# Attention of five tiles set 1 to 8 slots earlier in a hand-written schedule, with the resident routing weights

## What is computed

```
x += W_out[ diffattn(4 heads) | multi-scale pool ](rmsnorm(x) @ W_in)
x += PEER(rmsnorm(x))     # 8 heads, each: top 16 of 128*128 experts per token
x += sigmoid(rmsnorm(x) @ W_gate) * (p @ W_ple);  y = rmsnorm(x)
# PEER, for the indices idx that the routing scores choose:
h = gelu(einsum('td,thkd->thk', xb, u_tab[idx]))
out = einsum('thk,thkd->td', gate * h, v_tab[idx])
```

## Time and profile before

| | |
|---|---|
| Median of the three runs | 3161.15 us |
| Profiled execution, its own time | 3163.01 us |
| Its span, first to last instruction | 3160.7 us |
| PE / DVE / ACT / POOL busy | 74 / 71 / 30 / 42 % |
| DMA moved | 1260.27 MB, mean 399 GB/s |
| of it by the gather queue | 1133.76 MB, 87.2 % of 16 engines' time |
| of it by SyncE's queue | 122.82 MB |
| TensorE clock granted, mean | 0.870 |

### The profile page before, as it was taken

How to read it: one execution, slowest core, us unless ns; L and a number is a source line. 1 busy time by engine, 2 the same in 40 slices (tenths; PEclk the granted TensorE clock), 3 DMA queues, 4 the chain that set the end, 5 groups by cost and what they waited for, 6 DMA issues and landing times.

```text
span 3160.7 us, 53314 instructions
## 1 busy us (share of the span) xinstructions
PE 2345.9 (74%) x20876; PEld 935.8 (30%) x20876; DVE 2237.4 (71%) x5470; ACT 943.7 (30%) x2421; POOL 1319.9 (42%) x1143
## 2 busy tenths in 40 slices
PE   8789999577876877757876767576777676667656
PEld 4633333233333333213432222122222222222112
DVE  1466777668778789656667667587777777777775
ACT  1312333234435345222322212122332322222222
POOL 1024344334444334335555544344444444544442
PEclk9999999788898889878888888788898887889878
DMA  7679999999999999999999999999999999999996
GB/s 273 217 318 420 421 410 421 416 414 383 406 403 418 409 409 403 414 408 417 417 417 411 416 417 400 418 406 418 413 419 408 419 418 421 404 420 417 420 417 270
DMA packets 202034, 1260.27 MB, mean 399 GB/s; under 512 B 24048, under 2 KB 27400, under 8 KB 60848
## 3 DMA queue, kind: packets, MB, share of 16 engines
q0 software_dynamic: 159808, 1133.76, 87.2%
q1 hardware_dynamic: 40540, 122.82, 10.0%
q10 hardware_dynamic: 1436, 0.29, 0.0%
HBM read 1228.31 MB, written 28.65 MB: 398 GB/s over the span
## 4 chain that ended last, share of the span: by engine, by line
DMA 29%; PE 14%; DVE 8%; issue 3%; POOL 3%; DVEq 2%; ACT 2%; another core or an unknown queue 0%; POOLq 0%; ACTq 0%
DMA ring<-in_uv,idx 29%; PE sc L1007 7%; DVE ring L1887 4%; PE sc L1040 3%; POOL ring L2104 2%; PE route L982 1%; PE sc L1009 1%; DVEq L1897 1%; ACT diag L1402 1%; POOL front L2120 0%; ACT hgelu L1397 0%; PE sc L906 0%; DVE x L1936 0%; PE sc L1000 0%; PE sc L876 0%
## 5 line engine op out<-in xcount | busy, mean ns | idle before, releaser
L2104 POOL DMA_INDIRECT ring<-in_uv,idx x1056 | 1241.0, 1175 | 1647.6 <-PE sc L1009 1426.8
L1007 PE MATMUL sc<-ring,diag 32*32 32x512 f32 x8192 | 1232.3, 721 | 680.7 <-ACT diag L1402 617.6
L1887 DVE CUSTOM_DVE_ANT_0 ring<-ring,xn_cur 128x1024 f32<-128x1024 f32 x1056 | 1280.4, 1222 | 639.6 <-DMA ring<-in_uv,idx 604.1
L1009 PE MATMUL sc<-ring,diag 32*32 32x512 f32 x8192 | 1237.2, 721 | 0.0
L1007 PEld LDWEIGHTS sc<-ring,diag 32*32 32x32 f32 x8192 | 272.9, 117 | 1452.4 <-ACT diag L1402 1018.3
L1397 ACT ACTIVATE hgelu<-hdot 128x2 f32<-128x2 f32 x528 | 107.5, 204 | 1820.6 <-DVE hdot L1887 1740.3
L1402 ACT ACTIVATE diag<-gate_d,hgelu 128x32 f32<-128x32 f32 x1056 | 281.8, 314 | 21.2
L1009 PEld LDWEIGHTS sc<-ring,diag 32*32 32x32 f32 x8192 | 273.6, 117 | 5.8 <-issue 4.8
L564 PE MATMUL sc<-big,front 128*128 128x512 f32 x384 | 176.9, 604 | 3.3 <-DVE front L1515 2.9
L1397 ACT ACT_TABLE_LOAD x128 | 164.2, 1283 | 2.2
L982 PE MATMUL route<-big,xnT 128*128 128x256 f32 x560 | 134.4, 395 | 0.0
(11 more groups left out here) (310 smaller groups left out, 2362.9 us busy)
## 6 DMA issues: line engine op xcount, KB each, us to landing
front<-wqk_scratch SPq DMA_DIRECT2D x21, 1024.0 KB
ring<-in_uv,idx POOLq DMA_INDIRECT x1056
big<-in_w_in SPq DMA_DIRECT2D x8, 1024.0 KB, 13.7
wqk_scratch<-front SPq DMA_DIRECT2D x8, 1024.0 KB, 4.9
big<-wqk_scratch SPq DMA_DIRECT2D x8, 1024.0 KB
x<-x_scratch SPq DMA_DIRECT2D x12, 512.0 KB
ring<-in_wq_t POOLq DMA_DIRECT2D x10, 512.0 KB, 13.8
front<-in_x SPq DMA_DIRECT2D x8, 512.0 KB
```

What stands on the lines that cost most here:

```text
L1007: pe.matmul(sc[own, 0, :], diag[own, r, :], uv_rows[own, r, D:D + W4], start=opens_sum, stop=closes).then_inc(row_added[r], 1)
L1009: pe.matmul(sc[other, 1, :], diag[own, r, :], uv_rows[own, r, D + W4:2 * D], start=opens_sum, stop=closes).then_inc(row_added[r], 1)
L1887: dve.tensor_tensor_reduce(uv_rows[:, k % RING, 0:D], uv_rows[:, k % RING, 0:D], xn_cur[:, :], 1.0, 0.0, ALU.mult, ALU.add, hdot[:, n % 2, ...
L2104: pool.indirect_dma_start(uv_rows[:, k % RING, :], None, uv, bass.IndirectOffsetOnAxis(ap=idx[:, n % PH, j:j + 1], axis=0)).then_inc(row_i ...
```

## The change

The bases of tiles 3 to 7 go from 84, 101, 123, 145, 167 to 83, 99, 119, 139, 159: tile 3 follows tile 2 by 16 slots instead of 17, tile 4 follows tile 3 by 16 instead of 17, and tiles 5, 6 and 7 follow by 20 instead of 22. With tile 7, `BACK_FREE` goes from slot 190 to 182, and `C0` and all slots of the samples' attention by 8. `STREAMED` goes from 29 to 28, so head 28 is read from the resident weights and 20 loads of 1 MB are left of 21. Instructions, sizes and buffers are otherwise the same.

```
-STREAMED = 29
+STREAMED = 28
...
-    b = {2: 67, 3: 84, 4: 101, 5: 123, 6: 145, 7: 167}[t]
+    b = {2: 67, 3: 83, 4: 99, 5: 119, 6: 139, 7: 159}[t]
```

## The result

The changed kernel takes 3178.42 us (median of six runs, 3175.12 to 3180.57) against 3161.41 us for the kernel before: ratio 1.0053, 95% interval 1.0043 to 1.0063, so it is slower by 17 us. The forecast was 3166, with a range to 3177. The time lies above that range, near the 3174 of rival A. The profiled execution took 3177.8 us, its span is 3175.6 us, and the mean granted clock is 0.865.

A forecast was written before the change was run, and what follows sets the result against it. DMA bytes at 421 GB/s were taken to bound the kernel, plus dry stretches behind the projections where PE's debt outruns the ring; -2.5 us (megabyte) + 7.5 (PE debt) = +5.0, giving 3166 us, range 3153 to 3177.

The forecast's parts named there:

- rival A: Handovers and dense parts, tiles 3 to 7: all 12.5 us of new PE debt lost, 3 more in DVE; 3174 us, chance 0.36.
- What bounds the kernel: Whole kernel: DMA bytes at 421 GB/s set nine tenths of the time; the rest is lost while the engines run dry.
- The megabyte: One streamed head less: 1.05 MB fewer at 421 GB/s, -2.5 us, bounds 0 and -2.5.
- Resident heads, loads of q, k, u and bands: Resident loads eight slots sooner, attention loads one or two slots closer to their turn: both still covered, counted as nothing.
- Rival C: Slot 202: resident heads are late and head 28 waits for them, at worst a few us; chance 0.02.
- Work of PE in the handover: Slots of the projection halves, tiles 3 to 7: band and pool now ahead of the adds, debt 10.9 us per handover.
- The wait in the turn slot: Slot behind `turn_out`: turn waits for DVE to empty bank TA; 2.3 us for tiles 3, 4, 6, 1.0 for 5, 7.
- The 60%: Five handovers: share of the 12.5 us of added PE debt taken as lost, 7.5 us; bounds 0 and 12.5.
- The fixed point of 8.4 us: Each handover: PE debt the ring hides, if all above it were lost; from 54.3 us of debt and 12.1 lost.
- DVE: Attention region: same work in 99 slots instead of 107, share of DMA time 85% to 86%; nothing added, bound 3 us either way.

## Why the prediction was wrong

**What bounds the kernel: held.** The bytes set the pace, the late stretch ran at 420 against 421, and all of the change in time is in the stretches where the rate falls.

**The megabyte: held in the profile** (-2.2 against -2.5), unresolved by the times.

**Resident heads, loads of q, k, u and bands: held.** From slot 182 to slot 212 the kernel after ran at 413 GB/s and the kernel before at 412, so its 4.3 us more there are bytes, the samples' loads that moved up. The 420 expected there was not the rate of the kernel before either. Rival C didn't occur.

```profile
1260.10:1443.80 183.70, 119.44 (x1120) 43.78 (x1128) 119.40 (x299) 40.53 (x120) 72.65 (x68) 0.80 1.01 412
```
```profile
1275.80:1463.80 188.00, 120.43 (x1192) 48.12 (x1198) 115.27 (x286) 36.63 (x115) 82.21 (x74) 0.77 1.02 413
```

**Work of PE in the handover: the mechanism held, the size is open.** Band and pool ahead of the adds make POOL wait 9.0 us where the earlier trace rows had 7.30, and with the projection cut short the same schedule costs only 3 to 4 us. Of the 12.5 us of new debt the sum had put just 3.6 here and 8.9 in the turn slot. With the wait gone and the norm step moved, 5 us are left (1.0017), and 8 with the megabyte added back; the handovers then lose 2.1 us more than before, and the dense parts as much again. The turn itself is joined to the halves there too.

**The wait in the turn slot: this step failed.** It was priced at 2.3 and 1.0 us a tile, in sum 8.9, and measured 17.1. The wait as such was priced right: the turn started 1.5, 1.5, 0.3, 1.4 and 0.3 us behind the diagonals, where the step had 1.3 for tiles 3, 4 and 6 and none for 5 and 7. What was left out is that PE worked slowly behind its idle time. The five turns took 8.1 us instead of 5.2, and the adds behind them 4 us more than their 1.8 each. (This split into wait and slow work is read from the trace; no run had the wait without the lower clock.) The step took the turn's 1.04 from a row where half a projection stands right ahead of it and the clock is up; in the new place nothing stands ahead. The Trainium skill's page "TensorE: Matmul & The Clock Gate" (Part 1) says that the clock drops to half when PE has been idle for a while. The trace agrees: behind idle times of 5.12, 6.21 and 3.54 us the turn took 1.94, 1.94 and 1.90, behind 3.45 us 1.29, and behind 2.03 us 1.07. The length of the wait doesn't settle it by itself, though: with the turn ahead of the projection in the kernel before, a turn behind 3.51 us took 1.07, and in the changed kernel cut short one behind 2.25 us took 1.94. The kernel before had such slow adds too, ahead of the 1042.84 of the earlier trace rows:

```profile
1039.50:1042.80 3.30, 3.30 (x32) 0.68 (x32) 1.53 (x3) 0.16 (x1) 0.82 (x1) 0.54 1.02 418
```

That stretch lies just ahead of the earlier trace rows, and the prediction took 1.8 us for all adds. Taking off the 2.2 us that such adds cost before, the turn slots brought 14.9 us of debt and not 8.9.

**A rare step, put at nothing.** The norm step of slot 98 is DVE's own work and 2.35 us of standing still for ACT. It was in the trace of before, and the change brought the projection one slot closer to it and `turn_out` into its slot. The prediction looked only at the routing steps of the turn slot. Moving it gave back 5 us (1.0033 to 1.0017; 4.7 at tile 4 in the profile).

**The 60%: neither refuted nor shown.** With the measured turn slots the added debt is 12.5 + 6.0 = 18.5 us. 60% of it less 2.5 gives +8.6, and all of it +16; measured were +17. That looks as if all new debt were lost, which is rival A's condition. But about 5 of the 17 us went with the norm step, which is no work of PE in this sum. Without it the loss is 17 + 2.5 - 5 = 14.5 of 18.5 us by the times, and 15.6 - 4.7 = 10.9 by the lost DMA time of the attention (38.7 less 23.1): between 60 and 80%. The kernel with the turn one slot later says the same: its projections start -0.1, 1.4, 1.3, -0.1 and 1.1 us late (3.6 instead of 17.1), the turns' 5.2 us are joined to the halves instead, so it has 8.3 us less debt and gave back 6. With the turn slots and the norm step put right, and this share of it lost, the sum is 0.6 to 0.8 x 18.5 - 2.5 + 5 = +14 to +17. It is an estimate, since the share was found from the same time.

**Rival A: near the time, for other reasons.** A had a chance of 0.36 and 3174 us, 4 us from the measured time. It, too, had the turn slot at 8.9 and the norm step at nothing; that these two are missing (together 9 to 10 us) and that it takes all of the debt for lost and 3 us beside (5 to 8 us) nearly cancel, so a good part of its nearness is luck. The fixed point of 8.4 us is too simple for either: with the projection cut short the kernel before didn't get its 12.1 us back.

**DVE: within its bound.** 3 us either way was allowed, and A took 3. The dense parts between the handovers lost 9.5 us before and 12.2 after, 2.7 more; 1.8 of it show in tile 3's (740 to 764, beside 738 to 762 before).

**What makes up the 17 us,** by the ratios, each step a difference of two ratios and so good to some 5 us by their intervals: 6 for the wait in the turn slot and its clock (1.0053 to 1.0033), 5 for the norm step so close ahead of the projection (1.0033 to 1.0017), and the 5 that are left (1.0017), with the 2 to 3 of the megabyte on top, for band and pool joined to the halves and for fewer slots between handovers. The last two were not told apart.

## What to carry to other kernels

Before a producer and its consumer are set into neighbouring slots, ask what the engine does ahead of the wait: behind long work the wait is hidden and the clock is up, and behind nothing it is paid, and the work after it can run at half speed. Look for rare steps (a norm, a table load) in the slots that come together, and where the ring already runs dry, count most of the added delay of the engine that frees it as added time (here 60 to 80%). What is won at such a place can be lost again in the next dense part, so look at the whole. If a long piece of work bounds such a place, cut it into pieces, and not behind a wait; here that brought 0.15 to 0.2% in the old schedule and cost 0.2% in the new one.

## What the runs showed of the hardware

In all runs read here, waits on PE of 3.53 to 6.40 us nearly doubled the time of the turn behind them (1.04 to 1.90 and 1.94, at a granted clock of 0.50 to 0.52), and one of 6.21 us made a quarter of the projection 5.99 instead of 3.7 us (clock 0.61). Shorter waits went either way: 1.07 us behind 3.51, 1.29 behind 3.45, 1.94 behind 2.25, 1.07 behind 2.03. The projection behind the turn ran at 1.00 again.

The root of the norm step is one activation of 0.20 us on an engine that is 30% busy, and DVE stands 2.35 us for it, since ACT has to load a table for it. The timeline of ACT in the kernel before:

```profile
777.27 1.28 ACT L1376 ACT_TABLE_LOAD   x1
778.57 0.20 ACT L1376 ACTIVATE gst<-gst 128x1 f32<-128x1 f32 x1
778.78 1.28 ACT L1397 ACT_TABLE_LOAD   x1
```

A second load brings the GELU back, so ACT is taken for 2.8 us. The Trainium skill's page "ScalarE: Activation LUTs" (What ACT_TABLE_LOAD costs) gives 1283 ns for a load, whatever the table, and about 2.66 us for a switch with the drain; the trace agrees on the 1.28 us, and shows no drain apart from it.
